# MoBA keys of the decode stage turned by VectorE and scored in one pass of small tiles

## The chip, the core and the metric

The kernel runs on one core of one Trainium2 chip. The metric is the device time of one execution in microseconds (us); the kernel before takes 1144.55 us, the median of three runs. A core has five engines with a queue of instructions each: PE (TensorE, matmuls and transposes), DVE (VectorE), ACT (ScalarE), POOL (GpSimd) and SP (SyncE, which here only starts DMA transfers). Matmul results go to PSUM, eight banks of 128 partitions x 512 f32; everything else lies in SBUF, 128 partitions wide. Engines run side by side and wait for each other on counting semaphores.

## The reference, cut to what matters

One step of a hybrid decoder layer: a prompt of 256 tokens and 8 decode samples of 8 tokens each, with 2048 past positions per sample in pages of 128. Each sample has two attention mixers: MoBA (8 heads, keys in blocks of 256, the best 3 past blocks by the mean key, plus the own block) and NSA (compressed, selected and window attention). The change concerns the MoBA scores of the samples; the rest is computed as it was.

```python
def _moba(q, k, v, offset, slopes):
    ...
    kmean = jnp.mean(kp.reshape(B, nb, MOBA_BLOCK, H, HEAD_DIM).astype(jnp.float32), axis=2)
    own = ((offset + jnp.arange(T)) // MOBA_BLOCK)[None, :, None, None]
    gate = jnp.einsum('bthd,bnhd->bthn', q[:, :, :, 0].astype(jnp.float32), kmean)
    gate = jnp.where(jnp.arange(nb) < own, gate, NEG_INF)
    _, top = lax.top_k(gate, min(MOBA_TOPK, nb))
    ...
def _gathered_block_attn(q, k, v, idx, ok, offset, block, slopes):
    ...
        s = jnp.einsum('qkgd,qknsd->qkgns', q_c.astype(jnp.float32), ks.astype(jnp.float32)) * scale
        s = s - slopes[None, :, :, None, None] * (qpos - kpos).astype(jnp.float32)[:, :, None]
        ...
        p = _masked_softmax(s, mask, (-2, -1))
        return jnp.einsum('qkgns,qknsd->qkgd', p, vs.astype(jnp.float32)).astype(q_c.dtype)
def _compress(k, pe, w1, b1, w2, b2):
    ...
    return jax.nn.gelu(flat @ w1 + b1) @ w2 + b2
def _sample_layer(x, c, cache_moba_kv, cache_nsa_kv, cache_nsa_win, page_table, w, slopes_a, slopes_b):
    ...
    o_a = _moba(m['q_a'], full(cache_moba_kv, 0, m['k_a']), full(cache_moba_kv, 1, m['v_a']), past, slopes_a)
```

All arithmetic is in f32.

## The kernel before, in words

Three stages follow one another: the prompt and the projections (to about 261 us), the decode stage over the 8 samples (`decode_block`), and the back part (output projection and feed-forward network). Only the decode stage changes in its order of work; ahead of it the change adds a few small steps.

In `decode_block` every engine has a queue written out by hand: a preamble for sample 0, a hardware loop `Fori(0, NB - 1)` over 7 samples (`sequence(it, True)`), and a last `sequence(NB - 1, False)`. Within one pass, PE works on sample `it` in its first half, and mixes values of `it` with the NSA preparations of `it + 1` in its second. PE hands results over in a ring of four PSUM banks: the lists `STEADY`, `LAST` and `NSA_JOBS` fix which job takes which bank in which turn, `ring` makes PE wait until the bank's job four places earlier has been emptied, and `BY_DVE` says which jobs DVE empties (ACT does the others). The other four banks hold scores and sums for longer.

MoBA keys of one sample before: SP loads 16 pages of 128 positions x 512 into `Kr` (8 pages, two halves used twice). For each of four quarters PE turns four pages by 16 transposes of 128x128 into four ring banks (`key_transposes`, L1231), ACT and DVE copy the banks into `KTr` (`key_copy`; ACT 13 of the 16, DVE 3), and PE multiplies `KTr` with the staged queries `qa` (`key_scores`, L1242, four matmuls of 32 query columns x 512 keys, one for each pair of heads). DVE takes each quarter in `take_keys`: a sum for the gate (L1684), the addition of the position bias into `Sm` (L1685) and a maximum for each block (L1688).

Other names that the steps touch: `hidden_keys(q)` and `hidden_values` are the products of the compression MLP of `_compress` (L1207, 128x128 each, a sample has 48 for keys and 48 for values; `add_hidden` on DVE adds their parts, `middle` on ACT copies one part first, `gelu` follows). `segment_transposes`, `odd_segments` (ACT) and `segment_differences` (DVE) prepare the MLP's input `XT`; `relay_quarter` and `keep_quarter` are ACT copies of gathered NSA rows. `selected_transposes`, `selected_scores` and `take_selected` are the selected branch. `probabilities` turns the MoBA probabilities (`pmoba`) after ACT's eight exponentials, one for each block, and `moba_values` multiplies them with the pages of values.

A pass of PE before begins with `key_transposes(it, 0)` and 12 of the 24 products of `hidden_values(it, 0)`, and the copies, additions and takes of the other engines run beside these. In the preamble, DVE has for each quarter q a sum of weight taps (`add_taps`, L1668), two `segment_differences` and, after q = 1 and q = 3, `take_selected`.

## Time and profile before

| | us |
|---|---|
| time, median of three runs (lowest, highest) | 1144.55 (1143.61, 1147.43) |
| span of the profiled execution | 1140.6 |
| median time less that span | 3.95 |
| PE busy in that span | 1051.8 (92%) |
| DVE, ACT, POOL busy | 528.8, 544.4, 83.0 |
| decode: SP's first key page to PE's first transpose of keys in the loop | 27.47 |
| decode: one pass of the loop (the fourth of seven) | 60.20 |
| decode: the last sample | 41.02 |
| the back part, from the end of decode | 389.76 |

The profiled execution's own time is not given apart from its span, so sums below are made against the span, and 3.95 us are added to get from it to the median. A row of the timeline has the start, the time that the row takes, engine, source line, operation, what is written from what, shape, how many instructions it holds, and in brackets the idle time ahead of it with what ended it. Rows of one engine overlap at their ends: the time that a step costs on its engine is from its row's start to the next row's start.

### The profile page before, as it was taken

Reading aid. Unit: us, or ns where it says so; the run is one execution under the profiler, and the core shown is the slowest. Engines: PE = TensorE matmul, PEld = TensorE weight load, DVE = VectorE, ACT = ScalarE, POOL = GpSimd, SP = SyncE. Lnnn points to the kernel's source line nnn. Section 1 sums busy time; section 2 is a strip of 40 time slices with the busy share of each in tenths; the row PEclk is TensorE's granted clock in tenths of the full one; section 3 lists DMA queues with packets and bytes.
Section 4 is the critical chain, followed back from the end, with each engine's and each line's share of the span. In section 5 each row is a group of like instructions: output and inputs, shape, how many; then the busy total and the mean of one; then the engine's idle time right before and its main releaser. Section 6 shows DMA issues by size and latency. Waiting matters only on the chain. (4 is left out here: it accounts for less than half of the span.)

```text
span 1140.6 us, 25588 instructions
## 1 busy us (share of the span) xinstructions
PE 1051.8 (92%) x9297; PEld 912.2 (80%) x9297; DVE 528.8 (46%) x1174; ACT 544.4 (48%) x1069; POOL 83.0 (7%) x59
## 2 busy tenths in 40 slices
PE   7789996867999999999999999989999799999997
PEld 3578874656777787778787878769998799999997
DVE  1500015524545545463637363657457755555324
ACT  3422214645575666565756564561543444443223
POOL 1143410001000000000000100000000000000000
PEclk9799995867999999999999999988999899999999
DMA  9797776407666575758484846593565154443501
GB/s 331 214 309 246 246 255 224 178 37 279 221 212 231 193 242 179 269 159 284 134 305 132 310 147 221 182 268 103 176 201 166 41 181 147 147 147 148 185 0 47
DMA packets 129909, 219.51 MB, mean 192 GB/s; under 512 B 19348, under 2 KB 74129, under 8 KB 125058
## 3 DMA queue, kind: packets, MB, share of 16 engines
q1 hardware_dynamic: 124962, 185.14, 49.2%
q0 software_dynamic: 4896, 33.68, 8.0%
q8 instruction: 34, 0.56, 0.2%
q14 instruction: 17, 0.14, 0.0%
HBM read 210.46 MB, written 12.45 MB: 195 GB/s over the span
## 5 line engine op out<-in xcount | busy, mean ns | idle before, releaser
L103 PE MATMUL ps<-b_uH,b_slabH 128*128 128x320 f32 x480 | 152.3, 317 | 8.8 <-DVE b_uL L2341 5.3
L104 PE MATMUL ps<-b_uL,b_slabH 128*128 128x320 f32 x480 | 151.7, 316 | 0.0
L105 PE MATMUL ps<-b_uH,b_slabL 128*128 128x320 f32 x480 | 151.0, 315 | 0.0
L1207 PE MATMUL ps<-t_XT,t_slab 128*128 128x128 f32 x1024 | 142.6, 279 | 4.6 <-DVE t_XT L1655 3.5
L2229 DVE TENSOR_TENSOR b_slabL<-t_slab,b_slabH 128x2048 fp32r<-128x2048 f32 (+1 forms) x52 | 109.3, 2124 | 65.2 <-ACT b_slabH L2122 65.2
L1207 PEld LDWEIGHTS ps<-t_XT,t_slab 128*128 128x128 f32 x1024 | 127.2, 193 | 14.8 <-issue 10.6
L2122 ACT ACTIVATE b_slabH<-t_slab 128x2048 fp32r<-128x2048 f32 (+1 forms) x52 | 92.3, 1783 | 96.0 <-PE ps L105 90.6
L103 PEld LDWEIGHTS ps<-b_uH,b_slabH 128*128 128x128 f32 x480 | 93.4, 195 | 10.3 <-issue 6.6
L1504 ACT ACTIVATE t_KTr<-ps 128x512 f32<-128x512 f32 x152 | 82.1, 592 | 23.4 <-PE ps L1231 19.9
L104 PEld LDWEIGHTS ps<-b_uL,b_slabH 128*128 128x128 f32 x480 | 93.3, 194 | 0.0
L105 PEld LDWEIGHTS ps<-b_uH,b_slabL 128*128 128x128 f32 x480 | 93.1, 194 | 0.0
L1207 PE MATMUL ps<-t_XT,t_taps 128*128 128x128 f32 x512 | 83.9, 279 | 0.0
L1231 PEld LDWEIGHTS ps<-t_ident,t_Kr 128*128 128x128 f32 x512 | 55.7, 141 | 20.1 <-issue 13.2
L1207 PEld LDWEIGHTS ps<-t_XT,t_taps 128*128 128x128 f32 x512 | 69.5, 192 | 2.1 <-issue 1.4
L551 POOL DMA_INDIRECT t_nsa<-cache_nsa_kv,t_index x32 | 30.1, 941 | 509.8 <-ACT t_vsel L1504 293.0
L1231 PE MATMUL ps<-t_ident,t_Kr 128*128 128x128 f32 x512 | 62.4, 275 | 0.1
L1654 DVE TENSOR_TENSOR t_XT<-ps,t_XT 128x256 f32<-128x256 f32 x64 | 26.9, 420 | 75.6 <-PE ps L1182 50.5
L1504 ACT ACTIVATE t_relay<-t_nsa 128x512 f32<-128x512 f32 x64 | 36.7, 620 | 38.1 <-DMA t_nsa<-cache_nsa_kv,t_index 37.9
L103 PE MATMUL ps<-b_GH,b_slabH 128*128 (+1 forms) x176 | 54.5, 310 | 0.0
L105 PE MATMUL ps<-b_GH,b_slabL 128*128 (+1 forms) x176 | 54.4, 309 | 0.0
L104 PE MATMUL ps<-b_GL,b_slabH 128*128 (+1 forms) x176 | 54.4, 309 | 0.0
L237 POOL TENSOR_TENSOR t_f_L<-t_slab,t_f_H 128x2048 fp32r<-128x2048 f32 x10 | 46.0, 4600 | 102.1 <-ACT t_f_H L418 102.1
(388 smaller groups left out, 2080.9 us busy)
## 6 DMA issues: line engine op xcount, KB each, us to landing
t_Kr<-cache_moba_kv SPq DMA_DIRECT2D x132, 256.0 KB, 3.0
t_Vr<-cache_moba_kv SPq DMA_DIRECT2D x124, 256.0 KB, 5.7
t_slab<-w_ada SPq DMA_DIRECT2D x22, 1024.0 KB, 7.9
t_slab<-w_gu SPq DMA_DIRECT2D x22, 1024.0 KB, 5.2
t_slab<-w_in SPq DMA_DIRECT2D x17, 1024.0 KB, 6.5
t_slab<-w_down SPq DMA_DIRECT2D x11, 1024.0 KB, 5.0
t_slab<-cmp_w SPq DMA_DIRECT2D x2, 2048.0 KB
t_wkv<-cache_nsa_win SPq DMA_DIRECT2D x8, 512.0 KB, 3.2
```

Source lines behind the costliest of these rows:

```text
L103: pe.matmul(out, w_high, x_high, start=start, stop=False, **kw)
L104: pe.matmul(out, w_high, x_low, start=False, stop=False, **kw)
L105: return pe.matmul(out, w_low, x_high, start=False, stop=stop, **kw)
L237: pool.tensor_tensor(slabL[j % 2][:, :], slab[:, j % 2, :], slabH[j % 2][:, :].bitcast(F32), ALU.subtract).then_inc(w_split, 1)
L551: pool.indirect_dma_start(out=t["nsa"][:, q % 2, :], out_offset=None, in_=d["cache_nsa_kv"], in_offset=bass.IndirectOffsetOnAxis(ap=t["ind ...
L1207: return pe.matmul(out[:, P * j:P * j + P], taps(w, j, lp)[:, P * ht:P * ht + P], XT[:, w, lp, j, :, :].rearrange("p v i -> p (v i)"), sta ...
L1231: last = pe.transpose(bank[:, P * j:P * j + P], Kr[:, 4 * (q % 2) + j, P * hp:P * hp + P], ident[:, :])
L1504: return act.activation(dst, src, ACT.Copy)
L1654: dve.tensor_tensor(XT[:, :, lp, 0, :, :], seg[:, :, :, 0:NSEG:2], odd, ALU.subtract)
L2122: act.activation(slabH[:, s, 0:values], slab[:, s, 0:values], ACT.Copy).then_inc(w_high, 1)
L2229: dve.tensor_tensor(slabL[:, s, 0:values], slab[:, s, 0:values], slabH[:, s, 0:values].bitcast(F32), ALU.subtract).then_inc(w_split, 1)
```

## The change

Queries. A scaled copy `q_out` of all sample queries is made at the end of the first stage by one DVE instruction, stored to DRAM (`spill_q`) by four DMAs of SP in the prompt block, and for each sample brought back in four small DMAs (`load_queries`) in another layout; two ACT instructions (`pad_queries`) spread it into `qk`, with zeros between.

Keys. `Kr` holds all 16 pages of a sample. DVE turns each page in place, in blocks of 32x32, by one STREAM_TRANSPOSE of 128x512 (`turn_keys`, 16 a sample), one sample ahead: 4 a quarter in the preamble, and 2, 4, 2, 4 and 4 in a pass of the loop. The 64 transposes on PE, the 16 copies of banks and `KTr` are gone. `key_scores` is one run of 64 matmuls of 32x32 weights x 512 keys on the array's 16 tiles (4 row groups, 4 column groups, 4 that add up in each PSUM bank), into the four ring banks, at the end of the pass before. `take_keys` and the gate's sums (`gate_sums`) read these four banks; so the first four ring jobs of a pass (window, two `psel`, `pwin`) wait each for one `take_keys`.

Order. On PE, `segments(0)` and `selected_transposes(0)` of the next sample stand further ahead, and the products of the MLP's first quarter (`hidden_keys(0)`) behind the first quarter of values. On ACT, a one-element Gelu (`warm`) stands at the top of a pass, `relay_quarter(0)` ahead of the exponential of `Ss`, the first odd segments ahead of the eight exponentials, and one copy of selected keys with `keep_quarter(0)` between the fourth and the fifth of them. SP starts all 16 key pages of the next sample at the top of a pass; pages of values also wait for the gather of NSA rows.

```diff
+FRONT_JOBS = [("win", 0, 0), ("psel", 0, 0), ("psel", 1, 0), ("pwin", 0, 0)]
...
+STEADY = (FRONT_JOBS + cmp_jobs(0) + sel_jobs(0) + P_JOBS + cmp_jobs(1) + sel_jobs(1) + [("values", 0, 0), ("cout", 0, 0)]
+          + cmp_jobs(2) + sel_jobs(2) + cmp_jobs(3) + sel_jobs(3) + [("final", 0, 0)] + KEY_JOBS)
...
+BY_DVE = KEY_JOBS + [("values", 0, 0), ("cout", 0, 0), ("pown", 0, 0), ("final", 0, 0), ("pmoba", 0, 0), ("pmoba", 2, 0)]
...
+            def load_queries(it):
+                for i in range(4):
+                    sp.dma_start(qsrc[32 * i:32 * i + 32, :],
+                                 d["spill_q"][one(it), :].rearrange("b (a x) -> (b a) x", a=32)).then_inc(q_landed, 16)
...
+                sp.wait_ge(*keys_filled(it))
                 if more:
-                    for q in range(2):
-                        sp.wait_ge(filled, nth(it, ("key", q + 2, 3)))
+                    load_queries(it + 1)
+                    for q in range(4):
                         load_k(it + 1, q)
...
+                    sp.wait_ge(nsa_landed[1], it * 32 + 64)
+                    apart(sp, turns)
                     for q in (1, 2, 0):
                         sp.wait_ge(v_used, it * 4 + (q + 1 if q else 4))
                         load_v(it + 1, q)
...
+            sp.wait_ge(t["q_spilled"], 16 * 4)
+            load_queries(0)
+            for q in range(4):
                 load_k(0, q)
...
-            def key_transposes(it, q):
-                for hp in range(4):
-                    bank = ring(it, ("key", q, hp))
-                    if hp == 0:
-                        pe.wait_ge(k_landed[q % 2], it * 128 + 64 * (q // 2 + 1))
-                    for j in range(4):
-                        last = pe.transpose(bank[:, P * j:P * j + P], Kr[:, 4 * (q % 2) + j, P * hp:P * hp + P], ident[:, :])
-                    last.then_inc(filled, 1)
...
+            def key_scores(it, b):
...
+                banks = [ps[RING[i]] for i in range(4)]
+                pe.wait_ge(q_staged, b * N_STAGED + 6)
+                pe.wait_ge(keys_turned, b * 16 + 16)
+                apart(pe, turns)
+                for r in range(4):
+                    for hp in range(4):
+                        for i in range(4):
+                            rows32, c = slice(32 * i, 32 * i + 32), 32 * (4 * hp + r)
+                            last = pe.matmul(banks[i][32 * hp:32 * hp + 32, :].rearrange("p (g s) -> p g s", s=32),
+                                             qk[rows32, r, hp, :], Kr[rows32, :, c:c + 32], start=r == 0, stop=r == 3)
+                last.then_inc(filled, 4)
...
-                key_transposes(it, 0)
-                hidden_values(it, 0, range(0, 12), False)
...
                 bank = ring(it, ("win", 0, 0))
...
-                key_transposes(it, 1)
-                hidden_values(it, 0, range(12, 18), False)
...
+                hidden_values(it, 0, range(0, 4), False)
+
+                pe.wait_ge(cmp_act, it * N_ACT_CMP + 1)
+                compressed_keys(it).then_inc(keys_mm, 1)
...
+                wait_emptied(it, ("win", 0, 0))
+                pe.wait_ge(scores_taken, it * N_SCORE + 2)
...
-                key_transposes(it, 3)
...
+                hidden_values(it, 0, range(12, 24), True)
...
-                def segments(q):
-                    segment_transposes(it, it + 1, q, 0)
-                    segment_transposes(it, it + 1, q, 1)
...
                 moba_values(it, 0)
-                selected_transposes(it, it + 1, 0)
                 hidden_keys(it, it + 1, 0)
+                moba_values(it, 1)
+                segments(1)
+                selected_transposes(it, it + 1, 1)
                 compressed_values(it)
-                segments(1)
-                moba_values(it, 1)
+                hidden_keys(it, it + 1, 1)
...
                 segments(3)
                 selected_transposes(it, it + 1, 3)
                 final_transposes(it)
+                key_scores(it, it + 1)
+                selected_scores(it, it + 1, 1)
                 hidden_keys(it, it + 1, 3)
-                selected_scores(it, it + 1, 1)
...
+                    odd_segments(it, 0, 0)
+                    odd_segments(it, 0, 1)
                 act.wait_ge(max_done, it * N_MAX + 4)
...
+                    if more and n == 4:
+                        take_transposed_selected(it, 0)
+                        act.wait_ge(out_mm, it * N_OUT + 2)
+                        keep_quarter(0)
                     last = exp(Sm[:, MB * n:MB * n + MB], Sm[:, MB * n:MB * n + MB], t["mbias"][:, n:n + 1],
...
+            def turn_keys(b, pages):
+                for g in pages:
+                    if g % 8 == 0:
+                        dve.wait_ge(k_landed[g // 8], b * 128 + 128)
+                    dve.transpose(Kr[:, g, :], Kr[:, g, :]).then_inc(keys_turned, 1)
...
-            def take_keys(it, q):
-
-                bank = ps[2 + q % 2]
-                c = slice(512 * q, 512 * q + 512)
-                dve.wait_ge(scored, it * N_SCORE + AT_KEYS + q + 1)
-                dve.tensor_reduce(t["gate"][:, 2 * q:2 * q + 2], bank[:, :].rearrange("p (n s) -> p n s", n=2), AX.X, ALU.add)
-                dve.scalar_tensor_tensor(Sm[:, c], bank[:, :], cm[:, M_FAR + q:M_FAR + q + 1], cm[:, M_BIAS:M_BIAS + 512],
-                                         ALU.add, ALU.add).then_inc(scores_taken, 1)
-                dve.wait_ge(scores_taken, it * N_SCORE + AT_KEYS + q + 1)
...
+            def gate_sums(b, i):
+
+                dve.wait_ge(*keys_filled(b))
+                dve.tensor_reduce(t["gate4"][:, :, i], ps[i][:, :].rearrange("p (n s) -> p n s", n=NMB), AX.X, ALU.add)
+
+            def take_keys(b, i):
+
+                quarter = Sm[:, 0:PAST].rearrange("p (g i s) -> p i g s", i=4, s=32)[:, i, :, :]
+                dve.scalar_tensor_tensor(quarter, ps[i][:, :].rearrange("p (g s) -> p g s", s=32), cm[:, M_FAR + i:M_FAR + i + 1],
+                                         cm[:, M_BIAS:M_BIAS + 512].rearrange("p (g s) -> p g s", s=32),
+                                         ALU.add, ALU.add).then_inc(emptied_dve, 1)
+                dve.wait_ge(*keys_emptied(b, i))
+                dve.tensor_reduce(t["max4"][:, :, i], quarter.rearrange("p (n two) s -> p n two s", two=2), AX.XY, ALU.max)
...
-                add_hidden(it, 0, 0, ps[3])
-                add_hidden(it, 0, 1, ps[7])
-                key_copy(dve, dve.tensor_copy, it, 0, 0).then_inc(emptied_dve, 1)
+                add_hidden(it, 0, 0, H0)
+                add_hidden(it, 0, 1, H1)
...
+                    segment_differences(it, 0, 0)
+                    segment_differences(it, 0, 1)
+                add_hidden(it, 1, 1, S_WIN)
+                if more:
+                    turn_keys(it + 1, range(0, 2))
                 dve.wait_ge(cmp_act, it * N_ACT_CMP + 3)
...
+                    turn_keys(it + 1, range(2, 6))
                     segment_differences(it, 1, 0)
                     segment_differences(it, 1, 1)
+                    values_copy()
+                    turn_keys(it + 1, range(6, 8))
                     products_copy()
+                    turn_keys(it + 1, range(8, 12))
                     segment_differences(it, 2, 0)
                     segment_differences(it, 2, 1)
                     take_selected(it + 1, 0)
+                    turn_keys(it + 1, range(12, 16))
                     segment_differences(it, 3, 0)
                     segment_differences(it, 3, 1)
...
-                    take_selected(0, q // 2)
+                if q == 1:
+                    take_selected(0, 0)
+                turn_keys(0, range(4 * q, 4 * q + 4))
+            gate_sums(0, 0)
+            gate_sums(0, 1)
+            take_selected(0, 1)
```

### Order, PE at the top of a pass of the loop

PE, the first instructions of a pass, before (`t_ident,t_Kr` are the key transposes, `t_XT,t_slab` the products of the compression MLP, `t_wkv` the window keys; REGISTER_ALU and ISA are steps of a wait):

```order
L1231 MATMUL ps<-t_ident,t_Kr 128x128 x16
L1207 MATMUL ps<-t_XT,t_slab 128x128 x12
L1349 ISA
L1250 MATMUL ps<-t_hid,t_w 64x127 x4
L1256 MATMUL ps<-t_kaT_s,t_qa_cur 32x64 x4
L1258 MATMUL ps<-t_ksT_s,t_qb_cur 64x64
L1259 MATMUL ps<-t_kwT_s,t_qb_cur 64x64
L1164 REGISTER_ALU
L1353 ISA
L1355 MATMUL ps<-t_ident,t_wkv 128x128 x4
```

The four groups of key transposes and the twelve products stand ahead of the first score. The same place in the changed kernel:

```order
L1385 MATMUL ps<-t_ident,t_wkv 128x128 x4
L1240 MATMUL ps<-t_XT,t_slab 128x128 x4
L1389 ISA
L1283 MATMUL ps<-t_hid,t_w 64x127 x4
L1289 MATMUL ps<-t_kaT_s,t_qa_cur 32x64 x4
L1291 MATMUL ps<-t_ksT_s,t_qb_cur 64x64
L1292 MATMUL ps<-t_kwT_s,t_qb_cur 64x64
L1392 REGISTER_ALU
L1393 ISA
L1394 MATMUL ps<-t_ckT,t_qb_cur 64x127
L1197 REGISTER_ALU
```

The window transposes have moved to the very front, and four products instead of twelve stand between them and the MLP's second layer (`t_hid,t_w`); the key transposes are gone.

### Order, DVE in the preamble

DVE, from the weight taps behind the first quarter's differences to behind the first selected scores, before (`t_taps` is `add_taps`; `t_XT` the segment differences, four to a quarter; `t_Ss` and `t_smax` `take_selected`):

```order
L1668 TENSOR_TENSOR t_taps<-t_slab 128x512 x2
L1654 TENSOR_TENSOR t_XT<-ps,t_XT 128x2x128
L1655 TENSOR_TENSOR t_XT<-ps,t_XT 128x2x2x63
L1654 TENSOR_TENSOR t_XT<-ps,t_XT 128x2x128
L1655 TENSOR_TENSOR t_XT<-ps,t_XT 128x2x2x63
L1668 TENSOR_TENSOR t_taps<-t_slab 128x512
L1674 SCALAR_TENSOR_TENSOR t_Ss<-ps,t_cm 128x512
L1677 TENSOR_REDUCE t_smax<-t_Ss 128x32
L1668 TENSOR_TENSOR t_taps<-t_slab 128x512
L1654 TENSOR_TENSOR t_XT<-ps,t_XT 128x2x128
L1655 TENSOR_TENSOR t_XT<-ps,t_XT 128x2x2x63
L1654 TENSOR_TENSOR t_XT<-ps,t_XT 128x2x128
```

In the changed kernel:

```order
L1705 TENSOR_TENSOR t_taps<-t_slab 128x512
L1711 STREAM_TRANSPOSE t_Kr<-t_Kr 128x512 x4
L1705 TENSOR_TENSOR t_taps<-t_slab 128x512
L1691 TENSOR_TENSOR t_XT<-ps,t_XT 128x2x128
L1692 TENSOR_TENSOR t_XT<-ps,t_XT 128x2x2x63
L1691 TENSOR_TENSOR t_XT<-ps,t_XT 128x2x128
L1692 TENSOR_TENSOR t_XT<-ps,t_XT 128x2x2x63
L1705 TENSOR_TENSOR t_taps<-t_slab 128x512
L1717 SCALAR_TENSOR_TENSOR t_Ss<-ps,t_cm 128x512
L1720 TENSOR_REDUCE t_smax<-t_Ss 128x32
L1711 STREAM_TRANSPOSE t_Kr<-t_Kr 128x512 x4
L1705 TENSOR_TENSOR t_taps<-t_slab 128x512
```

Four page transposes now stand between the first quarter's taps and the second quarter's differences, and four more behind the first selected scores, ahead of the third quarter's; groups of four follow in the same way for the last two quarters.

## Rows read from the trace of the kernel before

**Rows 1.** Windows: start:end, length, PE, PEld, DVE, ACT, POOL busy, clock, DMA, GB/s.

```profile
261.20:288.67 27.47, 22.36 (x153) 19.64 (x153) 12.37 (x31) 14.65 (x32) 3.77 (x4) 0.81 0.89 321
468.65:528.85 60.20, 58.30 (x664) 47.23 (x662) 30.66 (x90) 38.00 (x89) 3.75 (x4) 1.00 0.65 222
709.82:750.84 41.02, 38.86 (x512) 31.11 (x510) 23.48 (x71) 22.70 (x56) 0.00 (x0) 1.00 0.61 187
```

**Rows 2.** Timeline of PE, keys of one sample, 482 to 493 us.

```profile
482.07 1.97 PE L1231 MATMUL ps<-t_ident,t_Kr 128*128 128x128 f32 x16
483.96 0.49 PE L1371 MATMUL ps<-t_Sc,t_c 64*128 64x127 f32 x2
...
487.27 2.06 PE L1242 MATMUL ps<-t_KTr,t_qa_cur 128*32 128x512 f32 x16
489.26 3.84 PE L1207 MATMUL ps<-t_XT,t_slab 128*128 128x128 f32 x32
493.04 1.09 PE L1386 MATMUL ps<-t_ident,t_Ss 128*128 128x128 f32 x8
```

**Rows 3.** Timeline of PE: single tiles of 64, and two row tiles.

```profile
202.36 2.00 PE L647 MATMUL ps<-t_ksT_p,t_qbT_p 64*128 64x256 f32 x16
...
478.32 1.07 PE L1361 MATMUL ps<-t_KTw,t_qb_cur 128*64 128x512 f32 x2
479.23 0.38 PE L1365 MATMUL ps<-t_ckT,t_qb_cur 128*64 128x127 f32 x2
```

**Rows 4.** Timeline of DVE: 512 columns, 256 columns, the chain to the mask.

```profile
266.43 1.29 DVE L1668 TENSOR_TENSOR t_taps<-t_slab 128x512 f32<-128x512 f32 x2
...
470.36 0.75 DVE L1661 TENSOR_TENSOR t_hid<-ps,t_mid 128x256 f32<-128x256 f32 x2
...
483.16 0.73 DVE L1685 SCALAR_TENSOR_TENSOR t_XT<-ps,t_cm 128x512 f32<-128x512 f32 x1
483.93 0.69 DVE L1688 TENSOR_REDUCE t_mbmax<-t_XT 128x2 f32<-128x512 f32 x1
...
487.50 0.28 DVE L1724 TENSOR_REDUCE t_imp<-ps 128x30 f32<-128x120 f32 x1
...
489.85 1.22 DVE L1741 TENSOR_TENSOR t_Ss<-t_Ss,t_sel_mask 128x1024 f32<-128x1024 f32 x1
...
491.57 0.42 DVE L1661 TENSOR_TENSOR t_hid<-ps,t_mid 128x256 f32<-128x256 f32 x1
```

**Rows 5.** Timeline of ACT: exponential, odd segments, kept rows, the middle copies.

```profile
498.09 0.49 ACT L1544 ACTIVATE t_XT<-t_XT,t_mbias 128x256 f32<-128x256 f32 x1
...
503.42 0.82 ACT L1504 ACTIVATE t_XT<-ps 128x256 f32<-128x256 f32 x2
...
506.37 0.61 ACT L1504 ACTIVATE t_vsel<-t_nsa 128x512 f32<-128x512 f32 x1
...
527.95 0.45 ACT L1504 ACTIVATE t_mid<-ps 128x128 f32<-128x128 f32 x2 [2.25 <-PE ps L1207]
```

**Rows 6.** Timeline of SP's queue: small loads, key pages.

```profile
174.23 5.21 SPq L608 DMA_DIRECT2D t_nsa<-nsa_kv_prompt  x8
...
261.20 8.15 SPq L1093 DMA_DIRECT2D t_Kr<-cache_moba_kv  x8
```

**Rows 7.** Landing times of the tile t_Kr, 261 to 270.4 us.

```profile
DMA to landing us min/median/max: 2.6/3.1/10.8
```

**Rows 8.** Landing times of the tile t_Vr, 271.5 to 274.7 us.

```profile
DMA to landing us min/median/max: 6.9/7.3/7.7
```

**Rows 9.** Timeline of PE: idle in the preamble and before the back part.

```profile
280.78 1.15 PE L1182 MATMUL ps<-t_ident,t_relay 128*128 128x128 f32 x8 [1.75 <-ACT t_relay L1504]
...
288.67 1.53 PE L1231 MATMUL ps<-t_ident,t_Kr 128*128 128x128 f32 x12
...
754.39 0.64 PE L103 MATMUL ps<-b_uH,b_slabH 128*128 128x320 f32 x1 [3.54 <-DVE b_uL L2247]
```

**Rows 10.** Windows, columns as in rows 1: the clock behind an idle stretch.

```profile
753.00:760.00 7.00, 5.61 (x21) 5.61 (x22) 7.00 (x8) 7.00 (x9) 0.66 (x1) 0.51 1.05 321
```

More of the change, by code:

```diff
@@ L1641, in _ @@
                 odd_segments(None, q, 1)
-                nsa_copy(act, copy, None, ("sel", q, 0)).then_inc(emptied_act, 1)
+                take_transposed_selected(None, q)
+            pad_queries(0)
             with act.Fori(0, NB - 1) as it:
```

356 lines of the change are left out of this document (180 added, 176 removed).

## The prediction, made before the changed kernel ran

> **What bounds the kernel now.** I read the windows by stage first: in one pass of the loop PE is busy 58.30 of 60.20 us, in the last sample 38.86 of 41.02, in the preamble 22.36 of 27.47 [rows 1]. So the loop is bound by PE, with 1.9 us of waits in a pass, and work taken off PE is time only as long as no wait takes its place. DVE is busy 30.66 of 60.20 us, ACT 38.00 [rows 1]: both have room on average, and what counts is whether they are in time at the single places where PE waits. Then I read PE's timeline for what a sample's keys cost, and the timelines of DVE and ACT for the length of each link in the chains that PE will wait for. The stage behind decode isn't touched.
>
> **The PE work, steady pass.** Four key transposes go: one takes 1.89 us from its start to the next row's [rows 2], so 4 x 1.9 = 7.6. The four scores go: two take 1.99 us [rows 2], so 4.0. The new key pass is 64 matmuls of 512 columns in two passes each, as the counts show (x16 for eight of them) [rows 2]. One tile alone takes (479.23 - 478.32) / 2 = 0.455 us for such a pass [rows 3]. Four column tiles run side by side: eight passes of four tiles take 1.0 us, not 3.6 [rows 2]. Two row tiles run side by side as well: sixteen passes of 256 columns take 2.00 us, half of what they would cost in a row at 0.23 each [rows 3]. No row shows 4 x 4 tiles. If all sixteen run together the pass costs 128 / 16 x 0.455 = 3.6 us; if rows pair only as rows 3 show, 128 / 8 x 0.455 = 7.3. I take 3.6, since column tiles scale in full up to four. PE's work then is 58.3 - 7.6 - 4.0 + 3.6 = 50.3 us.
>
> **The waits, steady pass.** I laid the changed queues of PE, DVE and ACT side by side with these links: a 512-column DVE operation 0.6 to 0.75, two 256-column ones 0.75, the chain from the importance sums to the next addition 491.57 - 487.50 = 4.07 [rows 4]; an exponential 0.49, two odd segments 0.82, a kept quarter or a bank's copy 0.5 to 0.6, two middle copies 0.45 [rows 5]; a product 3.78 / 16 = 0.236 [rows 2].
> (a) The window transposes, now first in the pass, go into the bank that `take_keys(0)` frees. Behind the last key product come the middle copies (0.45), two additions (0.75), three small memsets (0.3) and an addition of 512 columns (0.75): 2.3 us in which PE, in order, does nothing. Before, transposes of keys and products stood there.
> (b) The compressed score waits for the additions of the own scores, with little in between now: 0.9.
> (c) `pwin` waits for the third `take_keys`. DVE needs from the importance sums on 4.07 + an addition 0.35, gate sums 1.2, three additions with two maxima 3.5: about 9.4 with the hops; PE has the 30 products, 7.1, and the two `psel`, 1.0, and 0.2: a wait of 1.0.
> (d) The exponentials start behind the odd segments, and a copy and a kept quarter of 1.1 stand between the fourth and the fifth: `pmoba` 2 comes 1.5 late and `pmoba` 3 another 0.5: 2.0.
> (e) The differences of quarters 1 and 2 stand behind four or six page turns: at 0.6 a turn, `hidden_keys(1)` and (2) wait 0.4 and 0.9: 1.3.
> (f) The key pass needs all four ring banks and waits for the last copy: 0.7.
> Sum 8.2; the 1.9 of before go. A pass is 50.3 + 8.2 = 58.5, against 60.2: 1.7 us less, 7 x 1.7 = 11.9.
>
> **The price of a turn.** No row shows a STREAM_TRANSPOSE. The nearest are two-operand SBUF operations of 512 columns, 1.29 us for two [rows 4], so 0.6; below it, a fixed part and half the columns would be 0.4, as one of 256 columns takes 0.42 [rows 4]; above, two passes over the data would cost what 1024 columns do, 1.22 [rows 4]. I take 0.6. Each 0.1 us costs 16 x 0.1 in the preamble and about 0.4 in each pass through (c) and (e): 4.4 us. The Trainium skill (VectorE: DVE Perf Modes, The three transpose paths) gives 311 ns for a 128x128 block of 16-bit data on VectorE against 390 on TensorE; four such in a row would be 1.24 us a page, an estimate, which would speak against this change (about 1176 us, the second rival); no run here has shown it.
>
> **The last sample.** It loses 7.6 + 4.0 and has no key pass of its own; (b) and (c) are new, 1.9. 41.0 - 11.6 + 1.9 = 31.3: 9.7 less.
>
> **The preamble.** Nothing hides the turns of sample 0, and they stand between DVE's steps that PE waits for. SP first starts four query loads (eight small ones took 5.21 us, so 2.6), then pages at 8.15 / 8 = 1.02 each [rows 6]: the eighth at about 261.2 + 2.6 + 7.2 = 271.0. Pages started behind eight others landed after 7.3 us, the first eight after 3.1 at the median and 10.8 at worst [rows 7, 8]. I take 7, so 278; the ends are 274 and 282. DVE sits in `turn_keys` until then. Four turns 2.4, taps 0.6 and differences 1.4 put the second quarter's products at 282.9. Two sets of products and scores follow on PE: 2.8 + 1.0, to 286.7. Then DVE: `take_selected` 1.4, turns 2.4, taps 0.6, differences 1.4, taps 0.6, turns 2.4, taps 1.2, differences 1.4: 298.2. PE: 2.8 of products, 3.6 of key pass, 1.0 of scores, DVE beside it its last four turns: the key pass ends at 304.8. DVE: two gate sums 1.2, `take_selected` 1.4, an addition, memsets and the first `take_keys`, 1.8: PE's first instruction of the loop starts at about 309.3. Before it was 288.67 [rows 9]. So 20.6 us more.
>
> **The clock.** PE has granted 1.2 GHz (0.51) in the 7 us behind an idle time of 3.54, and kept its full clock across one of 1.75 [rows 9, 10]. In the new preamble PE stands still for some 9 us before the second quarter's products; they would run at the lower level, and 2.8 us of work at half speed cost up to 2.8 more: I take 2. In the loop, (a) is 2.3 us, between the two cases: from nothing to 2.8 in each pass; I take 3 for all passes.
>
> **Costs at nothing.** The stores of the queries by SP in the prompt block stand ahead of loads that have tens of microseconds; the two `pad_queries` and the Gelu load on ACT lie beside PE's products. All 16 key pages of the next sample are started at the top of a pass, some 30 us ahead of their turns. If that cover were gone, DVE would wait as in the preamble.
>
> **Sum.** -11.9 - 9.7 + 20.6 + 2 + 3 = +4.0 on a span of 1140.6: 1144.6. With the 3.95 between span and median, 1148.5 us, 0.35% above 1144.55. A measurement of this kernel can tell about 0.3%, 3.4 us, from no change, so 1141.1 to 1148.0 counts as the same.
>
> **Rivals.**
> First, faster: turns at 0.4 us, and the clock held throughout. Price -2 x 4.4 - 5 = -13.8: 1134.7 us. For it speaks that a turn has one operand where the rows have two; against it that the 512-column rows all stand at 0.67 to 0.75 whatever they do [rows 4]. From 0.43 a turn on it alone brings the time under 1141.1.
> Second, slower: turns at 1.2. Price 6 x 4.4 = 26.4: 1175 us. DVE then becomes what PE waits for in the second half of a pass.
> Third, slower: row tiles pair only. Key pass 7.3, eight times 3.7: +29.4: 1178 us. For it: no row has more than two row tiles at work. Against it: four column tiles do. The Trainium skill (TensorE: Matmul & The Clock Gate, Part 3: Packing small matmuls) states 10.6 times for 16 tiles of 512 columns, not 16; from it, an estimate, the pass would be 64 x 0.91 / 10.6 = 5.5 us and the time 8 x 1.9 = 15 more, 1164.
> Fourth: my waits (a) to (f) are read, 8.2 us in all; 1 us in a pass off is 7 us, and pages that land at 274 take 4 off: 1137 to 1159 from these alone. Not doing what it says, that is a key pass of four tiles at a time, would be 14.6 us a sample, 1236; the queue's order gives no reason for it.
>
> **How the numbers follow.** The forecast with its own spread, 1142 to 1155, has 0.42, about half of it at or below 1148.0. The first rival has 0.16; waits much shorter than read (below 1141) 0.07; waits longer or the clock lost in every pass, 0.15; turns near 1.2, 0.08; the key pass dearer than 5 us, 0.11; four tiles at a time, 0.01. Faster: 0.16 + 0.07 = 0.23. Same: 0.22 and a little of the others, 0.24. Slower: 0.53. The range leaves out the dear ends of the second and third rival and the lower edge of the first: 1135 to 1168.
>
> **What would show it.** Right: 16 turns at 0.6 us; DVE idle to about 278 and PE's first loop instruction near 309; the key pass at 3.6 us; some 2.3 us of PE idle ahead of the window transposes, released by DVE; 58 to 59 us between passes; 31 in the last sample. Wrong: a turn at 0.4 or 1.2, a key pass over 5 us, a loop clock under 1.00, or pages that land before 274 or after 282.

## The result, and the profile after

The changed kernel takes 1160.29 us (median of four runs, 1157.91 to 1164.66), the kernel before in the same session 1145.55: a ratio of 1.0134, with a 95% interval of 1.0103 to 1.0166. It is slower by 1.3%, where 0.35% was forecast. The profiled execution has a span of 1159.0 us, 18.4 more than before. Its own time is known, 1160.92 us, 1.9 above its span; if that holds for the kernel before too, its profiled execution lay some 3 us below the 1145.55, and that of the changed kernel lies 0.6 above its median, which is why the spans differ by more than the medians (14.7). By stages, each from the start of its first instruction to that of the next stage's:

| stage | before | after | difference | forecast |
|---|---|---|---|---|
| up to SP's first load of decode | 261.20 | 260.45 | -0.8 | 0 |
| preamble, to PE's first loop instruction | 27.5 | 51.3 | +23.9 | +22.6 with the clock |
| seven passes of the loop | 421.1 | 429.3 | +8.1 | -8.9 with the clock |
| last sample | 41.0 | 32.1 | -8.9 | -9.7 |
| back part | 389.8 | 385.8 | -3.9 | 0 |

So the preamble and the last sample came within 1.3 us of the forecast, and the miss sits in the loop. Rows of windows of the changed kernel: the preamble, the first, fifth and seventh pass of the loop, and the last sample (columns as in [rows 1]):

```profile
260.45:311.79 51.34, 30.85 (x283) 25.35 (x283) 26.64 (x59) 15.85 (x37) 3.76 (x4) 0.79 0.72 252
311.79:374.66 62.87, 54.86 (x695) 44.26 (x695) 38.86 (x107) 30.63 (x77) 3.75 (x4) 0.93 0.63 209
...
557.77:616.97 59.20, 51.21 (x694) 41.79 (x695) 38.85 (x107) 30.64 (x77) 3.75 (x4) 1.00 0.67 222
...
677.68:741.05 63.37, 55.46 (x694) 44.67 (x695) 38.79 (x107) 29.23 (x76) 1.87 (x2) 0.92 0.58 183
741.05:773.17 32.12, 27.72 (x414) 23.46 (x414) 17.84 (x61) 15.40 (x41) 0.00 (x0) 1.00 0.46 144
```

The fifth pass has its clock (the third number from the right, 1.00 for the higher of its two levels, 2.4 GHz, and about 0.5 for the lower, 1.2 GHz) at 1.00 throughout and takes 59.20; before, a pass took 60.20 at 1.00 [rows 1]. The other six have 0.92 to 0.97 and take 60.5 to 63.4 us; the four not shown took 60.7, 61.9, 60.5 and 60.7. PE's busy time grows as the clock falls (51.21 to 55.46) while its instructions stay the same: the same work runs slower.

PE's timeline in the undisturbed pass, the rows that carry waits, and two rows that bound a length:

```profile
557.77 0.65 PE L1385 MATMUL ps<-t_ident,t_wkv 128*128 128x128 f32 x4 [2.24 <-DVE t_XT L1730]
...
561.28 0.43 PE L1394 MATMUL ps<-t_ckT,t_qb_cur 128*64 128x127 f32 x2 [0.75 <-DVE t_Sw L1749]
...
574.25 0.29 PE L1422 MATMUL ps<-t_ident,t_Sc 64*127 64x64 f32 x1 [1.20 <-DVE t_XT L1730]
...
582.14 0.66 PE L1352 MATMUL ps<-t_ident,t_XT 128*128 128x128 f32 x4 [1.31 <-ACT t_XT L1580]
583.13 0.66 PE L1352 MATMUL ps<-t_ident,t_XT 128*128 128x128 f32 x4 [0.33 <-ACT t_XT L1580]
...
591.57 0.71 PE L1240 MATMUL ps<-t_XT,t_slab 128*128 128x128 f32 x4 [0.48 <-DVE t_cv L1842]
...
598.93 0.71 PE L1240 MATMUL ps<-t_XT,t_slab 128*128 128x128 f32 x4 [0.69 <-ACT t_PTs L1530]
...
606.40 4.45 PE L1275 MATMUL ps<-t_Kr,t_qk 32*32 32x512 f32 x128 [0.99 <-DVE t_oT_s L1872]
610.78 0.64 PE L1234 MATMUL ps<-t_PTs,t_qb_cur 128*64 128x512 f32 x1
```

In brackets stand (a) 2.24 for the window transposes, (b) 0.75 for the own scores, (c) 1.20 ahead of `pwin`, (d) 1.31 and 0.33 for the exponentials, (e) 0.48 and 0.69, (f) 0.99 ahead of the key pass: 8.0 in all, read as 8.2. The key pass takes 610.78 - 606.40 = 4.38 us, where 3.6 was taken.

The preamble on PE, then on DVE, then in SP's queue:

```profile
282.59 1.20 PE L1240 MATMUL ps<-t_XT,t_slab 128*128 128x128 f32 x4 [7.55 <-DVE t_XT L1692]
...
286.56 0.61 PE L1240 MATMUL ps<-t_XT,t_slab 128*128 128x128 f32 x4
...
311.79 1.11 PE L1385 MATMUL ps<-t_ident,t_wkv 128*128 128x128 f32 x4 [3.50 <-DVE t_XT L1730]
```

```profile
277.95 2.49 DVE L1711 STREAM_TRANSPOSE t_Kr<-t_Kr 128x512 f32<-128x512 f32 x4 [9.28 <-DMA t_Kr<-cache_moba_kv]
```

```profile
260.45 1.82 SPq L1132 DMA_DIRECT2D t_qsrc<-spill_q  x4
263.40 17.55 SPq L1121 DMA_DIRECT2D t_Kr<-cache_moba_kv  x16
```

DVE waits 9.28 us for the first eight pages and turns four of them in 2.49 us, 0.60 to 0.62 a page; PE stands still for 7.55 us before the second quarter's products, and for 3.50 before the loop, which begins at 311.79.

### The profile page after: what moved, and what is told of

Read it like the earlier page. It is cut to its first block and busy times, and to the rows that moved or that the text cites. A ratio compares the mean times of both kernels' runs of the same rounds, so it can differ in the third digit from the quotient of the medians.

```text
span 1159.0 us, 25924 instructions
## 1 busy us (share of the span) xinstructions
PE 1012.2 (87%) x9553; PEld 879.7 (76%) x9553; DVE 595.3 (51%) x1304; ACT 489.0 (42%) x982; POOL 83.0 (7%) x59
## 5 line engine op out<-in xcount | busy, mean ns | idle before, releaser
L1240 PE MATMUL ps<-t_XT,t_slab 128*128 128x128 f32 x1024 | 152.7, 289 | 16.9 <-DVE t_XT L1692 8.6
L1240 PEld LDWEIGHTS ps<-t_XT,t_slab 128*128 128x128 f32 x1024 | 134.4, 201 | 36.9 <-issue 16.1
L1711 DVE STREAM_TRANSPOSE t_Kr<-t_Kr 128x512 f32<-128x512 f32 x128 | 80.0, 676 | 9.3 <-DMA t_Kr<-cache_moba_kv 9.3
L1530 ACT ACTIVATE t_XT<-ps 128x256 f32<-128x256 f32 (+1 forms) x88 | 38.0, 439 | 60.0 <-PE ps L1214 48.0
L103 PE MATMUL ps<-t_f_H,t_uH 128*128 128x256 f32 (+1 forms) x168 | 47.8, 285 | 1.3 <-POOL t_f_L L237 1.3
L104 PE MATMUL ps<-t_f_L,t_uH 128*128 128x256 f32 (+1 forms) x168 | 47.2, 281 | 0.0
```

The lines of the kernel that those rows point to most:

```text
L103: pe.matmul(out, w_high, x_high, start=start, stop=False, **kw)
L104: pe.matmul(out, w_high, x_low, start=False, stop=False, **kw)
L1240: return pe.matmul(out[:, P * j:P * j + P], taps(w, j, lp)[:, P * ht:P * ht + P], XT[:, w, lp, j, :, :].rearrange("p v i -> p (v i)"), sta ...
L1530: return act.activation(dst, src, ACT.Copy)
L1711: dve.transpose(Kr[:, g, :], Kr[:, g, :]).then_inc(keys_turned, 1)
```

## The experiments

Five questions were open: what makes the clock fall in the loop, what sets the key pass, whether the preamble's growth is a matter of DVE's order, whether the waits come from where the forecast had put them, and what the turns cost in a steady pass. Where the row of a window stands for a pass, it goes from PE's window transposes of one pass to those of the next, unless it is said otherwise.

### Is it the idle stretch that lets the clock fall?

In a pass at the lower clock and in the undisturbed one, the same two steps right behind the wait (a), the second MLP layer and the window scores (PE's timeline; the first fence from the third pass, the second from the fifth):

```profile
436.85 1.12 PE L1283 MATMUL ps<-t_hid,t_w 128*64 128x127 f32 x8
...
440.19 1.91 PE L1397 MATMUL ps<-t_XT,t_qb_cur 128*64 128x512 f32 x2
```

```profile
559.25 0.66 PE L1283 MATMUL ps<-t_hid,t_w 128*64 128x127 f32 x8
...
561.55 1.02 PE L1397 MATMUL ps<-t_XT,t_qb_cur 128*64 128x512 f32 x2
```

1.12 against 0.66, and 1.91 against 1.02. Of the loop's seven falls, in six passes, six begin during (a) or within 2 us behind it; the seventh begins behind (d), in the seventh pass.

The first run fills (a) with work that is thrown away. Its edit:

```diff
             def sequence(it, more):
+                hidden_values(it, 0, range(0, 8), False)
                 bank = ring(it, ("win", 0, 0))
```

> The changed kernel with eight products of the next sample's first MLP slice issued a second time, ahead of the window transposes, where PE stands idle for 2.23 us in each pass; their sums are started anew right behind, so nothing else changes. In the changed kernel five or six of the seven passes run in part at the lower clock (mean clock of a pass 0.92 to 0.97) and take 61.3 us on the mean, the one at 1.00 takes 59.2. Theory A (the idle stretch at the top of a pass is what makes the clock fall): with 1.9 of the 2.2 us filled the clock stays at 1.00 in all passes, each takes 59.2, the loop loses 14.9 us, the time comes to about 1145. Theory B (the clock falls by something else in the pass: the key pass on 16 tiles, or the waits of 1.2 and 1.3 us further in): passes stay at 61.3 and the time at 1160.

Measured: 1158.39 us, ratio 1.0136 (1.0102 to 1.0169). The seven passes sum to 421.0 instead of 429.3, five of them 59.1 to 59.25 at a clock of 1.00, two of 62.5. One such long pass, and where the clock is low in it:

```profile
433.79:496.26 62.47, 56.26 (x711) 46.50 (x711) 38.96 (x107) 30.65 (x77) 3.75 (x4) 0.95 0.65 211
451.00:455.00 4.00, 4.00 (x25) 3.69 (x29) 1.95 (x12) 1.46 (x6) 0.00 (x0) 0.57 0.05 20
461.00:465.00 4.00, 4.00 (x45) 3.41 (x45) 3.12 (x8) 3.97 (x9) 0.00 (x0) 0.58 0.60 240
```

PE's timeline has these waits just ahead of the two low stretches:

```profile
450.28 0.29 PE L1423 MATMUL ps<-t_ident,t_Sc 64*127 64x64 f32 x1 [1.20 <-DVE t_XT L1731]
...
459.83 0.66 PE L1352 MATMUL ps<-t_ident,t_XT 128*128 128x128 f32 x4 [1.31 <-ACT t_XT L1581]
```

No fall begins at the top of a pass any more, which only theory A gives; but in two passes the clock now falls behind (c) and behind (d), and the loop gains 8.3 us and not 14.9. So the idle stretch at the top was the cause of the falls behind it, and the shorter waits further in can do the same. The key pass, which is the same in all passes, is not the cause. The time is not the 1145 that theory A gave: against the kernel before it stands where the changed kernel stood (1.0136 and 1.0134). In the profiled executions the 8.3 us are taken back by 2.8 in the preamble, 0.8 ahead of decode and 2.6 in the last sample and the back part. In the preamble the first eight pages of sample 0 were at hand 16.6 us behind SP's first key page instead of 14.6, and the loop began 51.2 us behind it instead of 48.4. In the six traces whose instructions are the same up to there, these pages came after 14.2 to 16.6 us, so that spread is no effect of the edits.

The second run moves the products instead of repeating them:

```diff
+                hidden_values(it, 0, range(0, 8), False)
                 bank = ring(it, ("win", 0, 0))
...
-                hidden_values(it, 0, range(0, 4), False)
...
-                hidden_values(it, 0, range(4, 12), False)
+                hidden_values(it, 0, range(8, 12), False)
```

> The changed kernel with the first eight products of hidden_values moved ahead of the window transposes (four from behind them, four from behind the window scores), not repeated. Theory A: the wait for the bank of take_keys(0) shrinks from 2.2 to about 0.4, the clock stays at 1.00, a pass takes 59.2 - 1.9 + up to 0.6 of new wait at the compressed probabilities = 57.3 to 57.9, the time about 1160 - 15 - 9 to 13 = 1132 to 1136. Theory B: only the wait goes, 61.3 - 1.3 to 1.9, the time about 1147 to 1151. If the wait only moves on to the next instruction that needs DVE, a pass stays at 59.2 and the time at 1145 with the clock held.

Measured: 1139.19 us, ratio 0.9959 (0.9928 to 0.9990). PE's timeline at the top of a pass, windows of an undisturbed pass and of the only disturbed one, and the wait ahead of the fall in the latter:

```profile
424.57 1.95 PE L1240 MATMUL ps<-t_XT,t_slab 128*128 128x128 f32 x16
426.97 0.65 PE L1386 MATMUL ps<-t_ident,t_wkv 128*128 128x128 f32 x4 [0.45 <-DVE t_XT L1730]
...
432.12 0.46 PE L1401 MATMUL ps<-t_Sc,t_c 64*128 64x127 f32 x2 [0.16 <-DVE t_Sc L1761]
```

```profile
426.97:484.63 57.66, 51.27 (x694) 41.74 (x695) 38.86 (x107) 30.63 (x77) 3.75 (x4) 1.00 0.70 228
484.63:543.91 59.28, 52.87 (x694) 43.18 (x695) 38.84 (x107) 30.63 (x77) 3.75 (x4) 0.97 0.68 223
```

```profile
507.43 0.66 PE L1352 MATMUL ps<-t_ident,t_XT 128*128 128x128 f32 x4 [1.31 <-ACT t_XT L1580]
```

The wait (a) is 0.45, a new one of 0.16 stands ahead of the compressed probabilities, and a pass takes 57.65; six of seven are undisturbed. The loop is 405.1, 24.2 less than in the changed kernel: 59.20 - 57.65 = 1.55 a pass is 10.9 of it, the clock the rest. The one fall left begins at about 509 us, behind (d) and not at the top of its pass. The pass came as theory A has it (57.3 to 57.9); the time lies 3 us above its 1132 to 1136.

The third run goes the other way: the kernel before, with a wait put where it had none.

```diff
             def sequence(it, more):
+                pe.wait_ge(cmp_act, it * N_ACT_CMP + 1)
+                apart(pe, turns)
                 key_transposes(it, 0)
```

> The kernel before, with one wait added: at the top of each pass PE waits for the second Gelu of the first MLP half before its first key transposes, about 2.6 us of idle in a place where it had none. No work changes. Theory A: the idle stretch alone brings the clock down behind it in most passes as in the changed kernel: a pass takes 60.2 + 2.2 (the idle, less what it saves later) + some 2 of lower clock = 64 to 65, the time about 1144.6 + 8 x 4 = 1175 to 1180, the clock of a pass 0.92 to 0.97. Theory B: only the idle, with the clock at 1.00: 8 x 2.2 = 18, the time about 1162.

Measured: 1183.24 us, one run. PE's first row of a disturbed pass and of the one undisturbed pass, and the windows of both, here from these rows to the next pass's:

```profile
558.69 3.36 PE L1231 MATMUL ps<-t_ident,t_Kr 128*128 128x128 f32 x16 [3.26 <-ACT t_hid L1542]
...
624.51 1.96 PE L1231 MATMUL ps<-t_ident,t_Kr 128*128 128x128 f32 x16 [3.31 <-ACT t_hid L1542]
```

```profile
558.69:624.51 65.82, 59.79 (x663) 48.62 (x663) 30.77 (x90) 37.67 (x88) 3.76 (x4) 0.98 0.59 200
624.51:687.84 63.33, 58.16 (x662) 47.23 (x663) 30.77 (x90) 37.93 (x88) 3.76 (x4) 1.00 0.61 206
```

The transposes that took 1.97 [rows 2] take 3.36 behind an idle stretch of 3.26, and six of seven passes have 0.97 or 0.98. So an idle stretch of some 3.3 us brings the clock down in most passes of a kernel that has no key pass on small tiles and no turns; in one pass the clock held across 3.31. On a stretch of 2.2 this run says nothing. The six disturbed passes take 65.0 to 65.8 us, the undisturbed one 63.3: 1.7 to 2.5 more, near the 2 that theory A took. The idle is dearer than expected (3.26, not 2.6), and the time lies above theory A's 1175 to 1180.

### What sets the key pass?

```diff
-                for r in range(4):
+                for h in range(2):
+                    for r in range(4):
...
-                            last = pe.matmul(banks[i][32 * hp:32 * hp + 32, :].rearrange("p (g s) -> p g s", s=32),
-                                             qk[rows32, r, hp, :], Kr[rows32, :, c:c + 32], start=r == 0, stop=r == 3)
+                                last = pe.matmul(banks[i][32 * hp:32 * hp + 32, 256 * h:256 * h + 256].rearrange("p (g s) -> p g s", s=32),
+                                                 qk[rows32, r, hp, :], Kr[rows32, 8 * h:8 * h + 8, c:c + 32], start=r == 0, stop=r == 3)
```

> The changed kernel with the key pass cut in two halves of eight pages: 128 matmuls of 256 columns instead of 64 of 512, the same products. The pass of 128 single passes took 4.39 us, 34 ns each, where 16 tiles side by side would give 3.64. Theory C (the 16 tiles work together as long as instructions come, one every 34 ns): twice as many instructions take 8.8 us, 4.4 us more in each of 8 samples, the time about 1195. Theory D (the tiles themselves are bound by columns, with 4.39 a matter of how well they pack): the same columns take 4.4 to 4.8 us and the time stays within 4 us of 1160.

Measured: 1173.23 us, one run. PE's timeline:

```profile
614.50 5.26 PE L1276 MATMUL ps<-t_Kr,t_qk 32*32 32x256 f32 x256 [0.99 <-DVE t_oT_s L1873]
619.69 0.64 PE L1234 MATMUL ps<-t_PTs,t_qb_cur 128*64 128x512 f32 x1
```

5.19 us with twice the instructions: neither 8.8 nor 4.4, but much nearer to theory D. With a part p for the columns and a part q for each single pass, p + 128 q = 4.38 and p + 256 q = 5.19 give q = 6.3 ns and p = 3.57 us; two lengths give two unknowns, so that the time grows in this way is taken and not shown. That p is near what sixteen tiles side by side should take, 3.64 from the 0.455 us of one [rows 3]; the 0.8 us on top would be 128 passes at 6.3 ns. The longer key pass explains 0.8 in each of eight samples, 6.5 of the 12.9 us over the changed kernel; much of the rest lies in this one execution. It came to decode 2.6 us later, and its first pass took 66.5, since PE stood still in the middle of the key pass:

```profile
366.57 3.97 PE L1276 MATMUL ps<-t_Kr,t_qk 32*32 32x256 f32 x189 [0.99 <-DVE t_oT_s L1873]
373.61 2.01 PE L1276 MATMUL ps<-t_Kr,t_qk 32*32 32x256 f32 x67 [3.06 <-issue]
```

In these 3.06 us the profile shows nothing that PE waited for, and its clock was at the lower level from 374.5 to 378 us. No other pass of this trace has such a stop.

### Are the preamble's 24 us the order of DVE's queue?

From here on each run stands on the variant with the products moved (1139).

```diff
                 if q == 1:
+                    turn_keys(0, range(0, 4))
                     take_selected(0, 0)
-                turn_keys(0, range(4 * q, 4 * q + 4))
+            turn_keys(0, range(4, 16))
             gate_sums(0, 0)
...
-            sp.wait_ge(t["q_spilled"], 16 * 4)
-            load_queries(0)
             for q in range(4):
                 load_k(0, q)
+            sp.wait_ge(t["q_spilled"], 16 * 4)
+            load_queries(0)
```

> On the variant with eight products moved to the top of a pass: the page turns of sample 0 stand behind all segment differences of the preamble (four of them ahead of the first selected scores), and SP starts the key pages ahead of the query loads. Nothing is left out. Theory P (the 23 us that the preamble grew are DVE's turns and its wait for pages standing in front of the differences): from SP's first load of decode to the first loop instruction of PE 51.3 us fall to 40 to 42, the idle 7.6 us ahead of the second quarter's products go, the time falls by 10 to 12 against the variant without it (1139), to 1127 to 1129. Rival Q (pages and turns themselves bound the preamble, wherever they stand: 16 pages, 9.9 us of turns, key pass): the first loop instruction comes at most 3 us earlier.

Measured: 1133.69 us, ratio 0.9908 (0.9875 to 0.9942), against 0.9959 without it. SP's first row of decode, and PE's rows of the key pass and of the first pass's window transposes, which have eight products ahead of them in this variant:

```profile
266.17 17.52 SPq L1121 DMA_DIRECT2D t_Kr<-cache_moba_kv  x16
```

```profile
297.35 6.03 PE L1275 MATMUL ps<-t_Kr,t_qk 32*32 32x512 f32 x128 [2.61 <-DVE t_Kr L1711]
...
307.88 0.65 PE L1386 MATMUL ps<-t_ident,t_wkv 128*128 128x128 f32 x4 [1.51 <-DVE t_XT L1730]
```

307.88 - 266.17 = 41.7 us, as theory P has it; with the old order it was 51.3 in the changed kernel, and 51.2 to 54.2 in the five variants that have it. About 3 us of the gain are the queries' loads behind the pages: SP's first key page came 2.95 us behind its first query load. The time falls by only 5.5 us at the medians, taken in different sessions, not by 10 to 12; the profiled executions came to decode at 257.50 us without this edit and at 266.17 with it, ahead of all that it touches. The stage's length shows the step better. What is left are the turns themselves: the key pass waits 2.61 for the last of them, and runs at the lower clock behind that (6.03 instead of 4.45).

### Do the waits come from where the forecast put them?

```diff
-                    if more and n == 4:
+                    if more and n == 6:
                         take_transposed_selected(it, 0)
-                        act.wait_ge(out_mm, it * N_OUT + 2)
-                        keep_quarter(0)
...
                 if more:
+                    act.wait_ge(out_mm, it * N_OUT + 2)
+                    keep_quarter(0)
                     relay_quarter(it, it + 1, 1)
```

> On the same variant: in a steady pass the copy of selected keys stands ahead of the seventh exponential instead of the fifth, and the kept quarter behind all eight. Theory S (the two copies of 1.0 us between the exponentials are what PE's third probability transpose waits for): its wait falls from 1.31 to 0.3, the fourth's rises from 0.33 to at most 0.9, a pass is 0.4 to 0.7 shorter: 57.0 to 57.2 instead of 57.64, the time 3 to 5 below 1139. Rival: PE waits for the exponentials by their start, behind the odd segments, and the pass stays within 0.2 of 57.64.

Measured: 1135.40 us, ratio 0.9920 (0.9890 to 0.9950); the five undisturbed passes 57.0. The third and fourth probability transposes on PE:

```profile
452.04 0.66 PE L1352 MATMUL ps<-t_ident,t_XT 128*128 128x128 f32 x4 [0.22 <-ACT t_XT L1580]
453.50 0.66 PE L1352 MATMUL ps<-t_ident,t_XT 128*128 128x128 f32 x4 [0.81 <-ACT t_XT L1580]
```

0.22 and 0.81 instead of 1.31 and 0.33: the copies between the exponentials were the wait (d), to the tenth.

```diff
                 take_keys(it, 0)
+                take_keys(it, 1)
...
                 gate_sums(it, 2)
-                take_keys(it, 1)
                 take_keys(it, 2)
```

> On the same variant: take_keys(1) stands right behind take_keys(0) at the top of a pass, where DVE is idle 1.5 us, instead of behind the selected mask. Theory T (pwin's 1.20 us are DVE's chain from the mask to the third take_keys, and the exponentials start by that chain as well): the 1.20 go, the exponentials start about 1.2 earlier, a pass takes 56.4 to 56.6 instead of 57.64, the time about 8 below 1139. Rival: the wait only moves on to the probability transposes (1.31 becomes 2.5), the pass stays at 57.6; or the own scores come late by the 1.4 (the wait of 0.75 grows) and it gets 0.3 longer.

Measured: 1130.77 us, ratio 0.9897 (0.9851 to 0.9943); passes of 56.3, six of seven at 1.00. The wait ahead of `pwin` (first row) is gone from PE's timeline, and the next one is no longer than it was:

```profile
442.71 0.32 PE L1422 MATMUL ps<-t_ident,t_Sc 64*127 64x64 f32 x1
...
450.63 0.66 PE L1352 MATMUL ps<-t_ident,t_XT 128*128 128x128 f32 x4 [1.31 <-ACT t_XT L1580]
```

So (c) was DVE's chain, and the exponentials hung on the same chain: 1.36 us a pass, the wait did not move on.

The three edits together:

> The three edits of this call together on the same variant. If their gains add: preamble 10 to 12, and 1.6 to 1.9 in each of seven passes, 12 to 13: the time 1139 - 23 = 1114 to 1118, 2.4% below the kernel before. If the loop's waits only move on among each other: 1125 to 1128.

Measured: 1112.72 us, ratio 0.9750 (0.9701 to 0.9798): the gains add (of a pass 57.65 - 55.68 = 1.97, where the two edits of the loop had given 0.63 and 1.36). All seven passes are undisturbed; one of them, and its second wait of (e):

```profile
359.40:415.08 55.68, 51.11 (x694) 41.76 (x695) 38.74 (x107) 30.49 (x77) 3.75 (x4) 1.00 0.71 237
```

```profile
397.04 0.71 PE L1240 MATMUL ps<-t_XT,t_slab 128*128 128x128 f32 x4 [0.70 <-ACT t_PTs L1530]
```

### What do the turns cost in a steady pass?

```diff
             def turn_keys(b, pages):
+                cols = P * 4 if isinstance(b, int) else 32
                 for g in pages:
...
-                    dve.transpose(Kr[:, g, :], Kr[:, g, :]).then_inc(keys_turned, 1)
+                    dve.transpose(Kr[:, g, 0:cols], Kr[:, g, 0:cols]).then_inc(keys_turned, 1)
```

> On the variant with all three edits: in the loop each page turn takes only the first 32 of the 512 columns, so the keys of samples 1 to 7 are left unturned in the other 480 (their scores are those of other keys); sample 0 is whole. DVE has some 8 us less to do in each pass, and nothing else changes. Theory U (in a steady pass the turns lie beside other work except for 0.5 to 0.7 us, four of them that stand ahead of the third quarter's differences): the wait of 0.70 ahead of that quarter's products goes, the other waits stay, a pass takes 55.0 to 55.2 instead of 55.68. Rival V (the turns still stretch the DVE chains at several places, 0.4 us of pass for each 0.1 us of turn): a pass takes under 54 us.

Measured: 1109.62 us, one run. A pass by its window (DVE is the third busy time), and PE's two waits of (e):

```profile
472.00:527.12 55.12, 51.11 (x694) 41.76 (x695) 31.06 (x107) 30.48 (x77) 3.75 (x4) 1.00 0.72 239
```

```profile
447.11 0.71 PE L1240 MATMUL ps<-t_XT,t_slab 128*128 128x128 f32 x4 [0.48 <-DVE t_cv L1843]
453.93 0.71 PE L1240 MATMUL ps<-t_XT,t_slab 128*128 128x128 f32 x4 [0.15 <-issue]
```

DVE has 7.7 us less to do, and the pass is 0.55 shorter, as theory U has it: the second wait of (e) falls from 0.70 to 0.15, the first, 0.48, stays, and all others too. The profile had put that second wait down to a copy of ACT, which stands as it was; it was the differences behind the turns. The first part of (e) was wrongly put down to the turns. In the changed kernel already, DVE was idle for 3.31 us between the turns and those differences, and waited for PE's segment transposes:

```profile
589.92 0.42 DVE L1691 TENSOR_TENSOR t_XT<-ps,t_XT 128x256 f32<-128x256 f32 x1 [3.31 <-PE ps L1214]
```

```diff
-                    turn_keys(it + 1, range(6, 8))
+                    turn_keys(it + 1, range(6, 10))
                     products_copy()
-                    turn_keys(it + 1, range(8, 12))
+                    turn_keys(it + 1, range(10, 12))
```

> On the same variant: four page turns instead of two in the gap that DVE has ahead of the compressed products' copy, and two instead of four behind it, ahead of the third quarter's differences. Theory U: the wait of 0.70 falls to about 0.1 to 0.2, a pass takes 55.1 to 55.2 instead of 55.68, the time 3 to 4 below 1113. Rival: the products wait for the segments' way over ACT anyway, and the pass stays at 55.6.

Measured: 1110.48 us, ratio 0.9718 (0.9677 to 0.9759); six passes of 55.1 with all columns turned (the first, with the clock low in part, took 56.5), with the first wait of (e) again at 0.48 and the second at 0.15:

```profile
452.96 0.71 PE L1240 MATMUL ps<-t_XT,t_slab 128*128 128x128 f32 x4 [0.15 <-issue]
```

The same 0.55 us, with whole turns: in a steady pass the 16 turns now cost no time that this comparison can show. This version is 2.8% faster than the kernel before.

## Why the prediction was right, and where it was off

**The direction and the range were right, the size was not**: 1160.3 lies in 1135 to 1168, but the slowdown is 14.7 us at the medians where 4.0 were worked out. That the time fell into the range is in part luck: its upper edge came from dear turns and from row tiles that only pair, and neither happened. The prediction had named a loop clock under 1.00 among the signs of being wrong, and that came, with passes of 59.2 to 63.4 us where it gave 58 to 59. By its steps:

- **The PE work.** Right but for the key pass: 4.38 us, not 3.6. The sixteen tiles do run together; what the sum lacked is 0.8 us, by the fit above 6.3 ns for each of 128 passes. That is 5.5 us over seven passes, and the third rival (7.3, tiles in pairs) is out. In this kernel the 16 tiles are worth a factor of 64 x 0.91 / 4.38 = 13.3. The Trainium skill (TensorE: Matmul & The Clock Gate, Part 3: Packing small matmuls) states 10.6, from which an estimate of 5.5 us for the key pass had been made; the run differs.
- **The waits.** 8.0 for 8.2, each at its place: (a) 2.24 for 2.3, (b) 0.75 for 0.9, (c) 1.20 for 1.0, (d) 1.64 for 2.0, (e) 1.17 for 1.3, (f) 0.99 for 0.7. The causes of (a), (c) and (d) were shown by taking them away. Of (e) only the second half was the turns. (b) and (f) were not tried.
- **The turn.** 0.60 us, as taken; the turns of 0.4 and of 1.2 in the first two rivals are out. The estimate of 1.24 us, which scaled by columns the 311 ns that the Trainium skill (VectorE: DVE Perf Modes, The three transpose paths) states for 128x128 in 16 bits, is out as well. The price given for a turn, 0.4 us of a pass for each 0.1, was too high: with nearly no turning a pass gains only 0.55 us (in the variant with the three edits).
- **The last sample.** 32.1 for 31.3: right.
- **The preamble.** 23.9 for 22.6: 8 pages at hand at 277.95 (278), the second quarter's products at 282.59 (282.9), the loop at 311.79 (309.3), of which the key pass is 0.8 and the clock 2 (from 282.59 to 286.56, three groups of products took 3.97 us, twice what they take at the higher level). The steps as the prediction lists them add up to 308.4; 0.9 of its 309.3 stands in none of them. That the growth is for the most part a matter of the order of DVE's and SP's queues, and not of pages and turns as such, the run with the turns moved back showed: 41.7 instead of 51.3, some 3 of it by the query loads.
- **The clock in the loop is the term that failed.** The sum had 3 us for all seven passes, and nothing to 2.8 for each; it was 429.3 - 7 x 59.2 = 14.9, in six passes of seven, with 1.3 to 4.2 in each. The rows had an idle stretch of 1.75 across which the clock held and one of 3.54 behind which it fell, and 2.3 lay between; that could have been priced as a case of its own, 7 x 2 us, with a chance near one half. It is most of the 14.4 by which the span's difference was missed: 11.9 of clock and 5.1 of longer passes in the loop (the key pass alone is 5.5), 2.1 more in preamble and last sample, less the 4.7 by which the stages ahead and behind came out shorter, which the change does not explain.
- **The back part** was 3.9 shorter, with no edit in it. Before, PE's clock fell a second time there (second row, 12.6 us behind the stage's first matmul), out of a stretch in which PE was busy without a break (first row), so an idle stretch is not the only thing behind which it falls:

```profile
760.00:767.00 7.00, 7.00 (x39) 5.91 (x38) 4.63 (x7) 2.79 (x3) 0.00 (x0) 0.99 1.06 299
767.00:781.00 14.00, 14.00 (x40) 10.62 (x39) 9.62 (x14) 2.57 (x4) 0.00 (x0) 0.52 0.33 75
```

In the changed kernel, at the same distance, it fell only for half as long:

```profile
789.40:803.40 14.00, 14.00 (x64) 12.01 (x63) 12.50 (x15) 3.66 (x5) 0.00 (x0) 0.76 0.36 81
```

In the ten other traces, with the same code in this stage, that second fall lasted 7 to 10.5 us. So I take the difference for one between executions and not for a term of the change; no kernel has two traces here that would show it.

## What to carry to other kernels

Work taken off the bounding engine is only worth what the engine doesn't then wait: list, in order, what the next instruction of that engine needs, and whether anything independent can stand ahead of it (moving eight products ahead of the wait was worth 24 us in the loop here). A wait of 2 us on TensorE is not priced by its length alone: it can bring the clock down behind it, so that such waits can cost nearly twice as much (here 16.9 us of waits at the top of seven passes, and 14.9 of clock, most of it behind them). Where a moved step enters a queue in a preamble, put it behind the steps that another engine waits for.

## What the runs showed of the hardware

- A STREAM_TRANSPOSE of 128x512 f32, in place, took 0.60 us in a row, no more than an addition of that width [rows 4].
- 64 f32 matmuls of 32x32 weights x 512 columns, on 16 tiles and four banks, took 4.38 us, and the same products as 128 matmuls of 256 columns 5.19; a straight line through the two gives 3.57 for columns and 6.3 ns for each of the 128 passes.
- Behind an idle stretch of 2.23 or 2.24 us at the top of a pass the clock fell to its lower level in five of six passes, for 3.5 to 7 us; behind 3.50, ahead of the first pass, for 10.5; behind 2.16, ahead of the last sample, not at all. With eight products there and 0.45 us idle, no fall came at the top; ahead of the first pass, where 1.3 to 1.5 us were left, one came in three of eight variants; behind the waits of 1.20 and 1.31 further in, the clock then fell in two of seven passes with the products repeated, and behind the second of them in one of seven with the products moved. Which passes fell was not settled.
